# Prompt attention on one Trainium2 core: scores two units ahead, a third set of score tiles, another order of copies

## What is computed

```python
s_s = jnp.einsum('bgrqd,bgqkd->bgrqk', qh, ks).astype(jnp.float32) * scale + bias_s
p_s = masked_softmax(s_s, (d_s >= 0)[:, :, None])
o_s = jnp.einsum('bgrqk,bgqkd->bgrqd', p_s.astype(vs.dtype), vs)
...
s_w = jnp.einsum('bgrqd,bkgd->bgrqk', qh, kw).astype(jnp.float32) * scale + tab[:, :, rel_bucket(d_w)]
p_w = masked_softmax(s_w, mask_w)
o_w = jnp.einsum('bgrqk,bkgd->bgrqd', p_w.astype(vw.dtype), vw)
g = gt.reshape(B, qb, 3, N_KV, REP).transpose(2, 0, 3, 4, 1)[..., None]
o = g[0] * o_c + g[1] * o_s + g[2] * o_w
```

## Time and profile before

| | us |
|---|---|
| median of 3 runs | 1267.23 (1264.92 to 1268.16) |
| the profiled execution's own time | 1266.38 |
| its span, first to last instruction | 1264.4 |
| TensorE, VectorE, ScalarE, GpSimd busy | 1221.5, 801.0, 572.5, 193.9 |
| mean granted TensorE clock | 0.989 of 2.4 GHz |

### The profile page before, as it was taken

The page is one execution under the profiler, slowest core; times in us unless marked ns, Lnnn a source line. Parts: engine busy times, 40 slices in busy tenths (PEclk is TensorE's granted clock), DMA queues, the critical chain, the costliest instruction groups (busy, mean ns, idle before and its releaser), DMA issues.

```text
span 1264.4 us, 25031 instructions
## 1 busy us (share of the span) xinstructions
PE 1221.5 (97%) x9304; PEld 1091.1 (86%) x9304; DVE 801.0 (63%) x1460; ACT 572.5 (45%) x1015; POOL 193.9 (15%) x379
## 2 busy tenths in 40 slices
PE   5999999999999999999988998999999999999997
PEld 3899999999999999997555667999999999978775
DVE  1787877742333366242587766588988888733466
ACT  2365555532221135343466655146555666523443
POOL 3000000000000036552292061031000000041000
PEclk9999999999999999999999999989999999999999
DMA  9935555556332335768242063633333233394563
GB/s 294 276 104 182 161 179 169 173 172 211 126 116 77 89 103 120 165 169 257 70 126 60 2 201 110 208 102 101 101 93 99 85 91 99 97 296 131 156 191 127
DMA packets 222195, 179.88 MB, mean 142 GB/s; under 512 B 48136, under 2 KB 199480, under 8 KB 222025
## 3 DMA queue, kind: packets, MB, share of 16 engines
q1 hardware_dynamic: 215201, 160.28, 43.2%
q0 software_dynamic: 6896, 18.35, 4.9%
HBM read 169.47 MB, written 13.35 MB: 145 GB/s over the span
## 4 chain that ended last, share of the span: by engine, by line
PE 86%; DVE 6%; ACT 4%; issue 1%; DMA 1%; DVEq 1%; SPq 0%; POOL 0%; ACTq 0%; POOLq 0%
PE ps L1500 30%; PE ps L367 26%; PE ps L1101 11%; PE ps L326 3%; PE ps L2990 2%; ACT AR L2378 2%; PE ps L1656 2%; PE ps L2978 1%; PE ps L2165 1%; PE ps L309 1%; PE ps L1708 1%; DVE AR L2548 1%; PE ps L2274 1%; PE ps L2182 1%; PE ps L447 1%
## 5 line engine op out<-in xcount | busy, mean ns | idle before, releaser
L1500 PE MATMUL ps<-UH,WH 128*128 128x288 f32 x512 | 152.2, 297 | 0.9 <-DVE RS L1588 0.9
L1500 PE MATMUL ps<-UH,WL 128*128 128x288 f32 x512 | 150.9, 295 | 0.0
L1500 PE MATMUL ps<-UL,WH 128*128 128x288 f32 x512 | 150.6, 294 | 0.0
L286 DVE TENSOR_TENSOR WL<-RAW,WH 128x1024 fp32r<-128x1024 f32 x61 | 76.2, 1250 | 114.6 <-ACT WH L282 112.5
L1500 PE MATMUL ps<-TB,WH 128*128 128x288 f32 x736 | 148.7, 294 | 0.0
L282 ACT ACTIVATE WH<-RAW 128x1024 fp32r<-128x1024 f32 x61 | 64.3, 1056 | 143.0 <-PE ps L367 128.6
L1500 PEld LDWEIGHTS ps<-TB,WH 128*128 128x128 f32 x736 | 118.1, 188 | 0.0
L1448 DVE TENSOR_TENSOR WL<-RAW,WH 128x512 fp32r<-128x512 f32 x144 | 99.1, 688 | 28.5 <-ACT WH L1443 28.4
L1500 PE MATMUL ps<-TB,WL 128*128 128x288 f32 x368 | 108.7, 295 | 0.0
L367 PE MATMUL ps<-UH,WH 128*128 128x288 f32 x480 | 103.9, 297 | 1.6 <-DVE WL L286 1.6
L1443 ACT ACTIVATE WH<-RAW 128x512 fp32r<-128x512 f32 x144 | 90.3, 627 | 29.0 <-PE ps L1500 24.2
(11 more groups left out here) (459 smaller groups left out, 2724.6 us busy)
## 6 DMA issues: line engine op xcount, KB each, us to landing
AW<-in_w_ada_dram SPq DMA_DIRECT2D x42, 512.0 KB, 4.5
RAW<-in_w_ffn_in_dram SPq DMA_DIRECT2D x72, 256.0 KB, 3.0
RAW<-in_w_ffn_out_dram SPq DMA_DIRECT2D x36, 512.0 KB, 3.8
RAW<-in_w_ffn_in_dram SPq DMA_DIRECT2D x34, 512.0 KB, 3.9
AR<-in_w_ffn_in_dram SPq DMA_DIRECT2D x18, 512.0 KB, 3.9
AR<-in_w_ada_dram SPq DMA_DIRECT2D x7, 1024.0 KB, 11.4
RAW<-in_w_ffn_out_dram SPq DMA_DIRECT2D x16, 448.0 KB, 3.8
AR<-in_w_ada_dram SPq DMA_DIRECT2D x14, 512.0 KB, 6.1
```

The lines of the kernel that those rows point to most:

```text
L286: nc.vector.tensor_tensor(WL[:, slot, :], RAW[:, slot, :], WH[:, slot, :].bitcast(F32), ALU.subtract).then_inc(split_done, 1)
L1500: mm = nc.tensor.matmul(acc(bank), W[g % 4][:, k * P:(k + 1) * P], R[:, k, :], start=(k == 0 and z == 0 and i in (0, 1, 3)), stop=(k == HK ...
```

## The change

- `X` gets a third set of four tiles (`XSETS` = 3). Two of the new tiles take a new tensor, `XS2`, that shares its place with `FACX` (used in another stage), two lie in `K1`. `xslot` counts modulo 3. The statistics get 12 columns each.
- Banks: scores of both branches go to banks 0 and 1, turned tiles of branch 0 to banks 4 and 5, of branch 1 to banks 2 and 3 (`TBANK`). So scores of one branch wait for biasing of the other one's tiles, and turns wait only for the copy of their own branch.
- Order: scores of unit u+2 are made in round u. PE has values(u-2, 1) first, then both turns, scores(u+2, 0), values(u-1, 0), scores(u+2, 1). ACT has the exponentials ahead of both copies. DVE biases one unit further ahead.
- `pt_on_act` is always true: the 12 copies of L2945 go to ACT.

Line numbers of the changed kernel are a few higher (L2155 is L2158, L2165 is L2168, L2177 is L2180, L2182 is L2185, L2378 is L2383, L2532 is L2536, L2541 is L2545, L2943 is L2949, L2949 is L2955).

PE where the stage begins, before: scores of unit 0 (L2155, four matmuls of 512 columns), compressed values, scores of unit 1, then both turns of unit 0, scores of unit 2.

The diff; of the bookkeeping all is shown but the statistics' columns:

```diff
@@ -155,7 +155,10 @@
         STT = sb("STT", [TT, 9 * NT])
-        FACX = sb("FACX", [P, HK * HT], F32R)
+        over_f = ExitStack()
+        FACX = sb("FACX", [P, HK * HT], F32R, over_f)
+        over_f.close()
+        XS2 = sb("XS2", [P, HK * HT])
         ADS = RS[:, 0:2 * ACOL]
@@ -2150,19 +2153,19 @@
                     i = 2 * br + g
-                    if u:
-                        pe.wait_ge(x_ready, 4 * (u - 1) + i + 1)
-                    nc.tensor.matmul(ps[:, i, 0:n], QT[64 * g:64 * g + 64, 4 + r, t * P:(t + 1) * P],
+                    if u or br:
+                        pe.wait_ge(x_ready, 4 * u + i - 1)
+                    nc.tensor.matmul(ps[:, g, 0:n], QT[64 * g:64 * g + 64, 4 + r, t * P:(t + 1) * P],
                                      QT[64 * g:64 * g + 64, (MKS, MKW)[br], 0:n], start=True, stop=True).then_inc(s_mm, 1)
...
                 r, t = step(u)
-                if u or br:
-                    pt_wait(pe, *((u, 0) if br else (u - 1, 1)))
+                if u:
+                    pt_wait(pe, u - 1, br)
                 for g in range(NG):
...
                     for k in range(t + 1):
-                        mm = nc.tensor.transpose(ps[:, 4 + g, k * P:(k + 1) * P], X[xslot(u, 2 * br + g)][:, k * P:(k + 1) * P],
+                        mm = nc.tensor.transpose(ps[:, TBANK[br] + g, k * P:(k + 1) * P], X[xslot(u, 2 * br + g)][:, k * P:(k + 1) * P],
                                                  IDN[:, :])
@@ -2184,7 +2187,6 @@
             scores(0, 0)
-            pe.wait_ge(cmp_d, CPT_READ)
             scores(0, 1)
@@ -2193,20 +2195,23 @@
             mm.then_inc(cmp2, 1)
+            scores(1, 0)
+            scores(1, 1)
             for u in range(NU + 1):
+                if u > 1:
+                    values(u - 2, 1)
                 if u == 1:
                     pe.wait_ge(vc_ready, 1)
+                    pe.wait_ge(cmp_d, CPT_READ)
                 if u:
                     turn(u - 1, 0)
-                if u > 1:
-                    values(u - 2, 1)
-                if u:
                     turn(u - 1, 1)
-                if u + 1 < NU:
-                    scores(u + 1, 0)
-                    scores(u + 1, 1)
+                if u + 2 < NU:
+                    scores(u + 2, 0)
                 if u:
                     values(u - 1, 0)
+                if u + 2 < NU:
+                    scores(u + 2, 1)
                 sample_cmp_pe(pe, u - 1)
@@ -2386,13 +2391,12 @@
             for u in range(NU + 1):
+                if 0 < u < NU:
+                    exps(u)
+                if u % 4 == 1 and u > 1:
+                    o_evac(act, u // 4 - 1)
                 if u:
                     pt_evac(act, u - 1, 0)
-                if u % 4 == 1 and u > 1:
-                    o_evac(act, u // 4 - 1)
-                if 0 < u < NU:
-                    exps(u)
-                if u:
                     pt_evac(act, u - 1, 1)
@@ -2525,11 +2529,11 @@
                 dve.wait_ge(s_mm, 4 * u + i + 1)
-                if u >= 2:
-                    dve.wait_ge(t_done, 2 * (u - 2) + i // 2 + 1)
-                elif u == 1:
+                if u >= XSETS:
+                    dve.wait_ge(t_done, 2 * (u - XSETS) + i // 2 + 1)
+                elif u == 2:
                     dve.wait_ge(natp_out, 32)
-                nc.vector.tensor_tensor_reduce(out=X[k][:, 0:n], in0=ps[:, i, 0:n], in1=GS[:, r + REP * (i % 2), (t + 1) * P - 1::-1],
+                nc.vector.tensor_tensor_reduce(out=X[k][:, 0:n], in0=ps[:, i % 2, 0:n], in1=GS[:, r + REP * (i % 2), (t + 1) * P - 1::-1],
                                                scale=1.0, scalar=TOP, op0=ALU.add, op1=ALU.min,
@@ -2547,14 +2551,14 @@

+            for i in range(4):
+                biased(0, i)
             for u in range(NU + 1):
...
                     weighted(u - 1)
-                if u < NU:
+                if u + 1 < NU:
                     for i in range(4):
-                        biased(u, i)
-                if u:
-                    pt_evac(dve, u - 1, 1)
+                        biased(u + 1, i)
                 sample_cmp_dve(dve, u - 1)
@@ -2681,7 +2685,9 @@
         PCX = v1["PCX"].rearrange("p (h t c) -> p h t c", h=NH, t=4)
-        X = [v[:, q * 512:(q + 1) * 512] for v in (v4["X"], v1["X2"]) for q in range(4)]
+        XSETS, TBANK = 3, (4, 2)
+        X = [v[:, q * 512:(q + 1) * 512] for v, n in ((v4["X"], 4), (XS2[:, :], 2), (v1["K1"][:, 3072:4096], 2), (v1["X2"], 4))
+             for q in range(n)]
         PT = [v.rearrange("p (g n) -> p g n", g=NG) for v in (v4["PT"], v1["PCX"])]
@@ -2920,10 +2926,10 @@
         def xslot(u, i):
-            return 4 * (u % 2) + i
+            return 4 * (u % XSETS) + i

         def pt_on_act(u, br):
-            return br == 0 or step(u)[1] == 3
+            return True

@@ -2940,9 +2946,9 @@
             if eng is nc.scalar:
-                nc.scalar.activation(PT[br][:, :, 0:n], ps[:, 4:6, 0:n], ACT.Copy).then_inc(pt_a, 1)
+                nc.scalar.activation(PT[br][:, :, 0:n], ps[:, TBANK[br]:TBANK[br] + 2, 0:n], ACT.Copy).then_inc(pt_a, 1)
             else:
-                nc.vector.tensor_copy(PT[br][:, :, 0:n], ps[:, 4:6, 0:n]).then_inc(pt_d, 1)
+                nc.vector.tensor_copy(PT[br][:, :, 0:n], ps[:, TBANK[br]:TBANK[br] + 2, 0:n]).then_inc(pt_d, 1)

```

More of the change, by code:

```diff
@@ L2691, in build @@
         VNW = AWF.rearrange("p (b c n) -> p b c n", b=NB, c=2)
-        NMX, SUM, WGT = MU[:, 0:8], MU[:, 16:24], MU[:, 32:40]
+        NMX, SUM, WGT = MU[:, 0:12], MU[:, 16:28], MU[:, 32:44]
         NM8 = MU[:, 48:80].rearrange("p (h t) -> p h t", h=NH)
```

## The result

| | before | after |
|---|---|---|
| median | 1267.6 us (10 runs, 1264.29 to 1269.27) | 1273.72 us (10 runs, 1270.08 to 1277.83) |
| ratio | | 1.0051, 95% interval 1.0035 to 1.0067 |
| profiled execution, its span | 1266.38, 1264.4 | 1270.08, 1268.4 |
| the stage, first scores to the sample's first transpose | 639.05 to 728.09: 89.04 | 637.30 to 733.22: 95.92 |

The changed kernel is 0.5% slower, above the forecast and above its range. In the profile the stage is 6.9 us longer, and 2.9 us of it come back outside (its start is 1.75 us earlier, and the half-clock period of the earlier trace rows at 779 us is not there).

The account below looks back on a forecast made before the run. PE, busy 97% of 1264.4 us, was taken as the bound. 3.0 - 0.1 - 2.75 = +0.1, with clock +1.0: 1266.38 + 1.1 = 1267.5, plus 0.85 to the median: 1268.3 us, range 1263.0 to 1272.0.

Parts of the forecast that it names:

- stage start to first turn: Selected and window attention, unit 0: first turn later by 5.8 us, as VectorE biases unit 1 before weighting unit 0.
- stage start to turn of unit 4: First head: 2.9 of the 5.8 us come back, turn of unit 4 at 673.0 instead of 670.00, +3.0 us.
- two middle heads: Units 4 to 12: a wait before window scores replaces the one removed; heads of 20.5 and 20.7 us, -0.1 us.
- end: After unit 12's turn: 2.5 us less scores work for PE; 14.05 us instead of 16.8, -2.75 us.
- clock: After a 4.1 us PE gap before the first turn, some 3.4 us of work begins at 1.2 GHz: +1.0 us.
- the walk: Going through each engine's fixed instruction list in the new order with the trace's durations; its sum for the stage: +0.1 us.
- the duration of scores: PE's scores of both branches take 1.91, 1.47, 1.07, 0.65 us for units of 512, 384, 256, 128 columns.
- the waits in front of scores beside units 4, 8 and 12: PE waits 1.5, 1.5 and 2.2 us for VectorE's biasing before window scores, once a head.
- Rival (3): Stage start: PE stays at 1.2 GHz for 10 us, first head grows 4 to 5 us; 1271.5 to 1272.5; chance 0.15.
- The copies: Twelve copies move from VectorE to ScalarE, 1.8 us more there per head; costed at nothing, under cover of PE's 4.4 us round.
- From profile to median: Whole kernel: the median of the runs stands 0.85 us above the profiled execution, added to 1267.5.
- Rival (2): Heads: PE packs better than its marks say, no wait at window scores; -5.0 us, 1262.2, heads near 18; chance 0.11.

Follow-up runs that it names:

- fill_all: Changed kernel plus unused identity transposes where TensorE waits before scores: 26 at the start, 5, 9 and 18 beside units 4, 8, 12; 1270.27 us.
- copies_only: Kernel before with only its 12 VectorE copies of turned tiles moved to ScalarE, old order and banks; 1264.66 us, ratio 0.9983 to before.
- copies_only_2: The kernel before with only its 12 VectorE copies moved to ScalarE, run once more; 1264.54 us, ratio 0.9976 to before.
- fill_start: Changed kernel plus only 26 unused identity transposes before unit 2's window scores; 1271.05 us, ratio 1.0044 to before.
- banks4_join: Changed kernel with scores in four banks and one run of eight between the two turns, turned tiles in banks 4 and 5; 1272.80 us.

## Why the prediction was wrong

| step | forecast | measured | off by |
|---|---|---|---|
| stage start to first turn | +5.8 us | 14.92 against 7.06: +7.9 | +2.1 |
| stage start to turn of unit 4 | +3.0 | 37.56 against 30.95: +6.6 | +3.6 |
| two middle heads | -0.1 | 43.34 against 41.29: +2.05 | +2.1 |
| end | -2.75 | 15.02 against 16.80: -1.8 | +1.0 |
| clock | +1.0 | in the rows above | -1.0 |
| stage (without the first row, which is part of the second) | +1.1 | +6.9 | +5.8 |

The rows of `fill_all`, without the clock's part, sort the misses better: the first head came out at +4.95 where the walk had +3.0, the middle heads at +2.1 for -0.1, the end at -3.45 for -2.75, and the clock at 3.3 for 1.0.

**The step that failed first** is the duration of scores. The walk took "scores of both branches 1.91, 1.47, 1.07, 0.65" from the old order, where eight matmuls stand in one run and their banks are free. In the new one they take 2.41, 1.92, 1.60 and 1.05: 1.9 us more in a head of four units. That fits the middle heads, at full clock 21.34 and 22.0 instead of 20.5 and 20.7, although the waits in front of scores beside units 4, 8 and 12 (0.60, 1.14, 2.20 us) were no longer than the 1.5, 1.5, 2.2 forecast. The duration is shown; that it is what lengthened the heads follows from this sum, not from an edit: with four banks and one run scores were short again, but other waits came. I named the place where scores wait, but counted a wait only once, at the first of the two tiles.

**The clock was right in kind and undersized.** The half-clock period at the start came, 650.0 to 656.8 us. I gave it 3.4 us of work; it lasted twice that. And the forecast put a 2.2 us wait beside unit 12 without asking what it does to the clock: 718.3 to 721.7 us at 1.2 GHz, 1.66 us in the turn alone. Together 2.4 to 3.5 us in place of 1.0. Rival (3) had this mechanism, at one place and for 10 us; the two places together had 10.2 us. Its bound, 1272.5, was too low: the misses of the start and of the scores lay on top.

**The start.** Weighting beside GpSimd was right (3.67 us from 646.66 to 650.33, forecast 4.0). Scores and biasing of units 0 and 1, which alternate through two banks, ended 9.4 us after the stage's start, not 7.9: VectorE waited 0.60 and 0.52 us for the window branch's scores of units 0 and 1, where the walk had 0.2 for a handover. At full clock (`fill_all`) the first turn is 7.4 us later than before, and 2.4 of them come back within the head, where the forecast had 5.8 and 2.9.

**The copies** on ScalarE cost little, as forecast: by its matmul marks TensorE waited 0.7 us for them in the stage, in front of the compressed part of the values (L2180). Its weight loads waited 6.4 us there, and how much of that cost time is not settled. But the step looked at ScalarE's queue alone. That they gain 2 to 3 us by themselves, and that the new order would lose 19 us without them, was not in it.

**The end** was right in kind, for a reason that is partly wrong: 15.02 us with its first turns at 1.2 GHz, 13.35 at full clock, against 14.05. The 2.5 us of scores saved are one unit too many. Behind unit 12's turn the old order had scores of two units, not three:

```profile
714.49 1.13 PE L2155 MATMUL ps<-AR 64*128 64x256 f32 x8
...
719.98 0.71 PE L2155 MATMUL ps<-AR 64*128 64x128 f32 x8
```

So scores save 1.07 us. Another 1.3 us is waiting: TensorE was idle for 2.1 us of this stretch before and for 0.75 after.

**From profile to median.** The profiled execution was the shortest of the ten; the median lies 3.6 us above it, where I added 0.85 from before. That is luck of one execution, and it hid 2.8 us of the loss from the profile. The executions differ by clock: 1270.1 us at 0.988, 1277.8 at 0.982. A wider spread than before is not shown: ten executions of the changed kernel range over 7.8 us, 35 of the kernel before over 8.4.

Rival (2), packing better, is excluded: no head came near 18 us. What stays open: what makes the clock fall after a wait in one execution and not in another; how the 3.6 us that remain at full clock divide between banks, split, lead and the later copies, though their places are known; and why `copies_only` has 5 us less at 1.2 GHz, outside the stage too.

## What to carry to other kernels

When a wait is removed by running further ahead, list what the new depth shares (here two banks for four tiles) and price each instruction in its new neighbourhood, not by its old mark: a wait between two matmuls of a run shows in the weight loads and nowhere in the matmul's idle time. Try each part of a bundled change alone; here the small part was the gain (1264.5 us, faster than both kernels), and the large one undid it. If the engine is already at 97%, many waits under 1 us can be cheaper than one of 2 to 3 us, which cost the clock as well here; waits of 1.1 to 1.3 us cost it in some of the profiles.

## What the runs showed of the hardware

- The clock falls in some executions and not in others of one kernel, at the same wait. `copies_only` and `copies_only_2` are one kernel; after the same two waits the first profile has a clock of 0.50 until 651, the second 1.00 throughout:

```profile
645.41 1.09 PE L2165 MATMUL ps<-IDN,AR 128*128 128x128 f32 x8 [0.83 <-ACT AR L2386]
647.62 1.97 PE L2165 MATMUL ps<-IDN,AR 128*128 128x128 f32 x8 [1.12 <-ACT AR L2941]
...
647.55 1.09 PE L2165 MATMUL ps<-IDN,AR 128*128 128x128 f32 x8 [0.83 <-ACT AR L2386]
649.75 1.09 PE L2165 MATMUL ps<-IDN,AR 128*128 128x128 f32 x8 [1.11 <-ACT AR L2941]
```

- It can fall while TensorE is busy. With TensorE's list the same up to the first turn, `fill_all` ran the 26 transposes in 3.06 us at 1.00, `fill_start` in 4.73 with a clock of 0.50 from 650 to 652 us. In the changed kernel it fell two us after the wait of 2.20 us had ended.
- A wait of little over 1 us can be enough: in `banks4_join` the clock was 0.50 at 696 to 702 us; it fell some three us after the end of a wait of 1.27 us, ahead of which TensorE had not waited for some 17 us. The Trainium skill, "TensorE: Matmul & The Clock Gate", section "A second HAM failure mode: psum-queue depth-cycling", says that frequent small pauses between groups of matmuls, as a kernel cycles through its PSUM banks, make the clock swing. `banks4_join` agrees, with two falls in the stage, at 675 and 695 us; the profile of the kernel before, with 15 short waits in front of its turns, stayed at 1.00 there.
